# An empty step between row transposes and the next projection job in an attention loop, with weight splits and closing additions moved apart

## The reference

```python
h = rms_norm(x, g_mix_norm[l])
z = h @ w_in[l]                       # q, compressed, selected and window keys/values, gates, zu, zv
...
o_attn = gates[0] * o_cmp + gates[1] * o_sel + gates[2] * o_win      # sparse attention, 8 heads
...
o_mix = zu * sv.reshape(B, S, MIX_WIDTH)                             # gMLP groups
o = concatenate([rms_norm(o_attn, g_out[l, :ATTN_WIDTH]), rms_norm(o_mix, g_out[l, ATTN_WIDTH:])])
x = x + o @ w_out[l]
h = rms_norm(x, g_ffn_norm[l])
x = x + square(relu(h @ w_ff1[l])) @ w_ff2[l]
```

## Time and profile before

| | us |
|---|---|
| median of three runs | 595.13 |
| the profiled execution's own time | 593.15 |
| its span on the core | 591.4 |
| PE busy | 570.4 (96%) |
| DVE busy | 440.8 (75%) |
| ACT busy | 358.7 (61%) |
| POOL busy | 127.1 (21%) |

### The profile page before, as it was taken

One profiled execution on the slowest core, in us unless ns is written; L12 is line 12 of the kernel. 1 busy time (PEld: TensorE's weight loads), 2 busy tenths in 40 slices (PEclk: granted clock), 3 DMA queues, 4 the chain that ended last, 5 costly groups with the idle time before them and its releaser, 6 DMA issues.

```text
span 591.4 us, 9215 instructions
## 1 busy us (share of the span) xinstructions
PE 570.4 (96%) x3433; PEld 497.8 (84%) x3433; DVE 440.8 (75%) x721; ACT 358.7 (61%) x644; POOL 127.1 (21%) x209
## 2 busy tenths in 40 slices
PE   8999999998899979989999999999999999999997
PEld 7777777887777867878999999999998888888886
DVE  3799881685778877756967675557699996898674
ACT  6866562638676775655683377743597656556551
POOL 1550000003343533420320201321023123020200
PEclk9999999999999999999999999999999999999999
DMA  8933247251112111001998966996879889976862
GB/s 307 335 99 130 86 147 279 72 212 40 63 45 71 37 37 37 2 1 36 182 198 206 169 208 150 189 199 167 203 137 190 207 171 207 245 137 224 187 203 108
DMA packets 25164, 87.56 MB, mean 148 GB/s; under 512 B 3024, under 2 KB 3312, under 8 KB 25120
## 3 DMA queue, kind: packets, MB, share of 16 engines
q0 software_dynamic: 9856, 35.38, 32.4%
q1 hardware_dynamic: 15120, 51.59, 25.1%
q10 hardware_dynamic: 144, 0.00, 0.0%
HBM read 84.87 MB, written 2.10 MB: 147 GB/s over the span
## 4 chain that ended last, share of the span: by engine, by line
PE 81%; DVE 8%; POOL 3%; DMA 3%; ACT 2%; issue 2%; SPq 1%; DVEq 0%; ACTq 0%
PE ps L427 23%; PE ps L429 23%; PE ps L428 23%; PE ps L2057 2%; PE ps L2076 1%; DMA xT<-in_xt 1%; PE ps L1927 1%; DMA pe_sb<-in_cmp_pe 1%; PE ps L1784 1%; DVE w_lo_sb L1203 1%; DVE ps L1505 1%; PE ps L2019 1%; PE ps L2018 1%; POOL rope_k L606 1%; DVE pt_sb L1528 1%
## 5 line engine op out<-in xcount | busy, mean ns | idle before, releaser
L1039 ACT ACTIVATE w_hi_sb<-raw 128x1024 fp32r<-128x1024 f32 x112 | 118.7, 1061 | 114.8 <-PE ps L429 93.3
L1566 DVE TENSOR_TENSOR w_lo_sb<-raw,w_hi_sb 128x1024 fp32r<-128x1024 f32 x112 | 137.1, 1225 | 64.7 <-ACT w_hi_sb L1039 64.5
L680 POOL DMA_DIRECT2D raw<-in_w_ff x64 | 55.4, 865 | 237.6 <-DVE w_lo_sb L1566 213.2
L427 PE MATMUL ps<-w_hi_sb,ht_hi 128*128 128x512 f32 x192 | 78.9, 411 | 9.4 <-DVE ht_lo L1232 7.1
L427 PE MATMUL ps<-w_hi_sb,a_hi 128*128 128x512 f32 x224 | 87.1, 389 | 0.0
L428 PE MATMUL ps<-w_lo_sb,a_hi 128*128 128x512 f32 x224 | 87.1, 389 | 0.0
L429 PE MATMUL ps<-w_hi_sb,a_lo 128*128 128x512 f32 x224 | 87.1, 389 | 0.0
L427 PE MATMUL ps<-ht_hi,w_hi_sb 128*128 128x256 f32 (+1 forms) x272 | 79.1, 291 | 0.0
L429 PE MATMUL ps<-ht_hi,w_lo_sb 128*128 128x256 f32 (+1 forms) x272 | 78.8, 290 | 0.0
L428 PE MATMUL ps<-ht_lo,w_hi_sb 128*128 128x256 f32 (+1 forms) x272 | 78.7, 290 | 0.0
L429 PE MATMUL ps<-w_hi_sb,ht_lo 128*128 128x512 f32 x192 | 75.7, 394 | 0.0
(11 more groups left out here) (239 smaller groups left out, 1138.7 us busy)
## 6 DMA issues: line engine op xcount, KB each, us to landing
raw<-in_w_ff POOLq DMA_DIRECT2D x64, 512.0 KB, 6.4
raw<-in_w_ff SPq DMA_DIRECT2D x48, 512.0 KB, 3.9
raw<-in_w SPq DMA_DIRECT2D x23, 512.0 KB, 4.5
xs<-in_x SPq DMA_DIRECT2D x8, 512.0 KB, 7.7
raw<-in_cmp_w SPq DMA_DIRECT2D x8, 512.0 KB, 4.3
xT<-in_xt SPq DMA_DIRECT2D x3, 512.0 KB, 8.8
raw<-in_w_c SPq DMA_DIRECT2D x4, 304.0 KB, 2.8
out_y<-xs SPq DMA_DIRECT2D x2, 512.0 KB, 3.1
```

Source lines behind the costliest of these rows:

```text
L427: pe.matmul(out, l_hi, r_hi, start=start, stop=False)
L680: pool.dma_start(raw[:, n % RAW, :], (w_ff1, w_ff2)[stage - 1][k, q], accum_op=ALU.add, max_dma_last_dim=8192).then_inc(raw_added[n % RAW] ...
L1039: act.activation(w_hi_sb[:, FS[j], :], raw[:, j, :], ACT.Copy).then_inc(w_hi, 1)
L1566: dve.tensor_tensor(w_lo_sb[:, FS[j], :], raw[:, j, :], w_hi_sb[:, FS[j], :].bitcast(F32), ALU.subtract).then_inc(w_lo, 1)
```

## The change

The steps of the jobs are set anew: after each of the six row transposes in the loop (steps 1, 35, 41, 47, 53, 59) one step has no job, and the last projection runs in steps 61 to 64 instead of 56 to 59. The weight splits `hi` and `lo` move to steps with equal distances. `combine` is cut into its two additions, the second one step later; three readers of its result move one step with it. The sum of squares and the row scaling of tile 1's MLP input move to step 60.

```diff
 JOBS = {("mix", 3, 0): 1}
-JOBS.update({("mixo", t, 0): 2 + 4 * t for t in range(NT)})
-JOBS.update({("mixo", t, 1): 18 + 4 * t for t in range(NT)})
+JOBS.update({("mixo", t, 0): 3 + 4 * t for t in range(NT)})
+JOBS.update({("mixo", t, 1): 19 + 4 * t for t in range(NT)})
...
-                if v in (24, 40, 56):
+                if v in (25, 41, 57):
                     inverse_root("attn", v // 16 - 1, 1)
...
-                if s == 2:
-                    hi(22)
-                if s == 10:
-                    hi(23)
-                if s in (19, 22, 26, 28):
-                    hi(24 + (19, 22, 26, 28).index(s))
-                if s in (20, 36, 52):
+                if s in (3, 7, 19, 23, 27, 31):
+                    hi(22 + (3, 7, 19, 23, 27, 31).index(s))
+                if s in (21, 37, 53):
                     act.wait_ge(o_evac, 2 * (s // 16))
                     norm_sum("attn", s // 16 - 1, scr[:, 0:AW])
...
-                if s in (48, 58):
-                    t = (s - 48) // 10
+                if s in (48, 60):
+                    t = (s - 48) // 12
...
-            def combine(t, q):
+            def combine(i, e):
-                i = 2 * t + q
+                t, q = i // 2, i % 2
...
+                if e == 0:
+                    dve.wait_ge(co_done[t // 2], t % 2 + 1)
+                    dve.wait_ge(back_done, 2 * i + 2)
+                else:
+                    dve.wait_ge(o_step, i + 1)
+                dve.tensor_tensor(o, o, ps[:, 7, :].rearrange("p (h e d) -> p h e d", e=2, d=HD)[:, :, e, :], ALU.add
+                                  ).then_inc(o_evac if e else o_step, 1)
...
-                if s == 3:
-                    lo(22)
-                if s == 11:
-                    lo(23)
-                if s in (20, 23, 27, 29):
-                    lo(24 + (20, 23, 27, 29).index(s))
+                if s in (4, 8, 20, 24, 28, 32):
+                    lo(22 + (4, 8, 20, 24, 28, 32).index(s))
...
-                if s >= LAG + BACK and (s - LAG - BACK) % 8 == 7:
-                    combine((s - LAG - BACK) // 16, (s - LAG - BACK) // 8 % 2)
-                if s in (41, 48, 53, 57):
-                    ffn_rows(s // 50, {41: 0, 48: 1, 53: 0, 57: 1}[s])
+                for e in range(2):
+                    i, at_group = divmod(s - LAG - BACK - e, 8)
+                    if i >= 0 and at_group == 7:
+                        combine(i, e)
+                if s in (41, 48, 53, 60):
+                    ffn_rows(s // 50, {41: 0, 48: 1, 53: 0, 60: 1}[s])
```

More of the change, by code:

```diff
@@ L204 @@
 JOBS = {("mix", 3, 0): 1}
-JOBS.update({("mixo", t, 0): 2 + 4 * t for t in range(NT)})
-JOBS.update({("mixo", t, 1): 18 + 4 * t for t in range(NT)})
-JOBS.update({("attn", 0, 0): 34, ("attno", 0, 0): 36, ("attn", 1, 0): 40, ("attno", 0, 1): 41, ("ffn", 0, 0): 45,
-             ("attno", 1, 0): 46, ("ffn", 0, 1): 50, ("attno", 1, 1): 51, ("attn", 2, 0): 55,
-             ("attno", 2, 0): 56})
+JOBS.update({("mixo", t, 0): 3 + 4 * t for t in range(NT)})
+JOBS.update({("mixo", t, 1): 19 + 4 * t for t in range(NT)})
+JOBS.update({("attn", 0, 0): 35, ("attno", 0, 0): 37, ("attn", 1, 0): 41, ("attno", 0, 1): 43, ("ffn", 0, 0): 47,
+             ("attno", 1, 0): 49, ("ffn", 0, 1): 53, ("attno", 1, 1): 55, ("attn", 2, 0): 59,
+             ("attno", 2, 0): 61})
 def steps_of(k):
@@ L1536, in coefs @@
                 dve.reciprocal(coef[:, t, hs, b:b2 + 1], psum_p[:, t, hs, b:b2 + 1]).then_inc(coef_made, 1)
-            def combine(t, q):
-                i = 2 * t + q
+            def combine(i, e):
+                t, q = i // 2, i % 2
                 o = o_sb[:, t, 256 * q:256 * q + 256].rearrange("p (h d) -> p h d", d=HD)
-                src = ps[:, 7, :].rearrange("p (h e d) -> p h e d", e=2, d=HD)
-                dve.wait_ge(co_done[t // 2], t % 2 + 1)
-                dve.wait_ge(back_done, 2 * i + 2)
-                dve.tensor_tensor(o, o, src[:, :, 0, :], ALU.add).then_inc(o_step, 1)
-                dve.wait_ge(o_step, i + 1)
-                dve.tensor_tensor(o, o, src[:, :, 1, :], ALU.add).then_inc(o_evac, 1)
+                if e == 0:
[5 more added lines that the diff above has]
+                                  ).then_inc(o_evac if e else o_step, 1)
             def add(kind, t, h):
@@ L1567, in unit_lo @@
                                   ALU.subtract).then_inc(w_lo, 1)
-            for w in range(NV + LEAD + LAG + BACK):
+            for w in range(NV + LEAD + LAG + BACK + 1):
                 s = w - LEAD
```

## The result

The changed kernel takes 584.39 us (median; 584.14 to 585.47), the kernel before beside it 594.83 us (594.32 to 595.3): a ratio of 0.9828, 95% interval 0.9811 to 0.9845. Forecast were 590.1 us and 586.2 to 594.5. The profiled execution of the changed kernel took 584.51 us, its span is 582.8 us.

The account below looks back on a forecast made before the run. TensorE, busy 570.4 of the 591.4 us span, was taken as the bound. Terms of -5.5 us, with 0.5 given back, made 588.15 us; 1.98 us added for the median gave 590.1 us, range 586.2 to 594.5.

Parts of the forecast that it names:

- 1.98 us: Median of the runs above the profiled execution in the kernel before, added to 588.15 us to give 590.1 us.
- step 35: Transpose in attn tile 0: a new wait behind the split now at step 32, 1.1 us, between 0 and 1.5.
- all waits covered: Rival: readings find engines free, only tile 0's new waits and under 2 us elsewhere stay; -8.5 us, 586.6 us; chance 0.17.
- the empty steps: Behind the loop's transposes: a step without a job gives TensorE 2.56 us of cover in tile 2, 2.77 in tile 3.
- the end of the loop: Steps 60 to 63: three waits, 1.1 us, go with chunks in 61 to 64; 0.1 us added for the last addition.
- Steps 47 and 1: Waits for transpose readings: 2.29 us falls to 1.4 at step 47, 1.97 to 1.85 at step 1.
- Tile 0 and tile 1: Tile 0: GpSimd waits of 1.9 us go, three waits for additions, 2.1 us, come; tile 1: 2.2 us for 2.33.
- The allowance of 0.5 us: Given back on the summed gain of 5.5 us, since less idle time leaves VectorE less in which to catch up.
- The fall at 222 us: Clock drop to 0.50 behind step 47's wait of 2.29 us: gone once the wait is cut, 1.65 us back.
- GpSimd late by the splits: Rival: TensorE waits for each scaling pair blocked by a split, 4.6 us of gain lost; 594.2 us; chance 0.17.
- Late reciprocals behind the additions: Rival at VectorE's even steps: thirteen additions expose 0.6 us each, 7.8 us against 5.5 saved; 597.4 us; chance 0.08.
- The clock's return: Rival: the clock drop comes back behind another wait, 1.65 us; 591.8 us; chance 0.08.

Follow-up runs that it names:

- combine whole: The changed kernel with combine in one piece again and its three readers one step earlier; 584.68 us, ratio 0.9853 to the kernel before.
- the one with the split a step later: The changed kernel with every job behind step 1's transpose and the six weight splits one step later; 586.42 us, ratio 0.9885 to the kernel before.
- splits alone: The kernel before with only the new steps of the weight splits; 597.71 us, ratio 1.0070 to the kernel before.
- old splits: The changed kernel with the six weight splits at their old steps; 587.98 us, ratio 0.9907 to the kernel before.
- late jobs alone: The kernel before with the new table only for jobs from step 34 on; 585.73 us, ratio 0.9870 to the kernel before.
- the kernel with 2.75 us: The changed kernel with step 47's transpose moved to 48, so its projection follows at once; 588.86 us, ratio 0.9915 to the kernel before.
- jobs alone: The kernel before with the whole new job table, splits and combine unchanged; 587.05 us, ratio 0.9882 to the kernel before.
- first half alone: The changed kernel with the jobs from step 35 on as before; 594.59 us, ratio 1.0013 to the kernel before.
- mirror: The changed kernel with the eight mixo projections and the six weight splits one step earlier; 584.58 us, ratio 0.9841 to the kernel before.
- combine alone: The kernel before with only combine cut into two additions a step apart, its three readers one step later; 594.01 us, ratio 1.0004.
- old parity: The changed kernel with the eight mixo projections one step earlier, ending at odd steps, splits unmoved; 590.85 us, ratio 0.9936 to the kernel before.

## Why the gain was twice the forecast

Two steps failed. Most of the waits came as forecast, but the prediction carried 1.98 us over to the changed kernel that were falls of the clock (2.1 us of the 5.7 missing), and it charged TensorE with a wait at step 35 that isn't there (1.1 us of the 2.7 missing in idle time). The first alone decides: without the 1.98 us the range would have been 584.2 to 592.5 us, which holds the 584.39, and the rival "all waits covered" had -8.5 us for the profiled execution, where -8.6 was measured.

**What bounds it, the empty steps, the end of the loop: right.** From step 48 to the tail the named waits are gone (forecast 0.3 us left), the idle time fell from 4.74 to 1.18 us, 1.04 of it the `combine` wait of the tail in both kernels. Steps 47 and 1: forecast 1.4 and 1.85 us, measured 0.92 and 1.67. The reading behind step 47's transpose ended 3.9 us from its last matmul, not 4.2, and TensorE came for it 3.0 us from there, not 2.8.

**The step that failed in the waits: step 35.** "I take 1.1 us in all here" for the split of step 32. There is no wait. VectorE and TensorE:

```profile
193.68 1.52 DVE L1199 SCALAR_TENSOR_TENSOR w_lo_sb<-raw,gcol_sb,w_hi_sb 128x512 fp32r<-128x512 f32 x2
...
197.65 0.60 PE L1779 MATMUL ps<-ident,o_sb 128*128 128x128 f32 x4
...
199.57 0.69 DVE L1228 TENSOR_TENSOR ht_lo<-ps,ht_hi 128x512 fp32r<-128x512 f32 x1
...
200.40 0.47 PE L427 MATMUL ps<-w_hi_sb,ht_hi 128*128 128x512 f32 x1
```

The reading ends at 200.26, 0.14 us before TensorE comes. VectorE is busy without a gap from the split on, as I had said, but its queue is in the order of the steps, and TensorE itself isn't free earlier. I charged VectorE's backlog to TensorE without setting it against the cover that I had just counted (2.56 us; here TensorE came 2.3 us behind the transpose); the whole reading took 2.2 us. How near it is shows in the run with combine whole (0.21 us) and in the one with the split a step later (0.37 us).

**Tile 0 and tile 1: size.** The three new waits were there, 0.59, 0.60 and 0.38 us (1.57) for 2.1; GpSimd's 1.9 us went as forecast. First stretch 3.24 us for 3.9, second 2.08 for 2.2. In tile 1 TensorE waited for VectorE's `_lo` (0.63, 0.50, 0.31 us) and then for ScalarE's `ot_keep` (0.18, 0.18, 0.29), never for a closing addition. That the shift of the projections would cost 2.1 us was seen; that the splits' new steps are its condition was not. Without them and the cut of `combine` the same table is 2.7 us slower in its median, some 1.8 at full clock; without the table they cost 3.8 us. I priced split by split and had not asked how far each stands from the next addition.

**Idle time in sum:** -6.5 us where the terms had -3.8 (steps 0 to 15 -0.6 for 0; 16 to 31 -0.25 for -0.1; 32 to 47 -2.1 for -0.4; from 48 on -3.6 for -3.3).

**The allowance of 0.5 us** "in which VectorE catches up" had no row, and went the wrong way. TensorE's busy time in the loop fell from 108.46 to 105.99 us; the clock is 1.7 of it. Some of the other 0.8 is in the first matmul behind a wait, which shows 0.50 us for 0.39; the rest stays open. Before the loop and in the tail 0.4 us were added. Profiled execution against profiled execution that is -8.6 us: 593.15 to 584.51.

**The step that failed in the clock: one fall was counted, and there were two.** The fall at 222 us went, 1.65 us as forecast. But I added 1.98 us, the median over the profiled execution, to the changed kernel as if it were an overhead. It is no property of the launch: the changed kernel's median is 0.1 us below its profiled execution. This is 2.1 us of the 5.7 missing, the rest are the 2.7 of idle time, the 0.5 of allowance and the 0.8 less 0.4 us. The first three executions of the kernel before have no clock on record, but in the later sets 43 of 71 have the clock of two falls, and the two profiled ones had one. So the 1.98 us were most likely a second fall, behind the waits in tile 0, that the profiled execution happened not to have. By the executions at full clock, of different sets, the two kernels lie some 7 us apart (591.4 to 591.6 against 584.1 to 584.5, one 585.5); the other 3 of the 10.4 us between the medians fit two falls of the clock that went. In the last set, where the changed kernel had one fall in each execution that counts, the gain was 8.3 us by the medians.

**Readings.** VectorE's idle share in the four stretches of the earlier trace rows is 36, 20, 23 and 29%, not 18 to 30; the first stretch sums to 3.96 us, not 3.9; in the third the terms add up to a gain of 0.4 us, which is written as -0.4. None of it changes the forecast by more than 0.1 us.

**The rivals.** The nearest was "all waits covered", 586.6 us; the covered step 35 is its mechanism. GpSimd late by the splits: the scaling beside a split does take longer, and nobody waits for it. The timeline of the changed kernel:

```profile
185.52 1.60 POOL L670 TENSOR_SCALAR p_sb<-p_sb,coef,glog 128x256 f32<-128x256 f32 x2
...
186.09 1.57 DVE L1199 SCALAR_TENSOR_TENSOR w_lo_sb<-raw,gcol_sb,w_hi_sb 128x512 fp32r<-128x512 f32 x2
```

1.60 us against 1.09. I had all six pairs 0.93 us longer, and found three longer by 0.5 (1.60, and 1.41 twice in tile 0 for 0.88); the splits themselves took 1.52 to 1.67 us beside a scaling and 1.41 without. That it would cost TensorE 4.6 us is refuted. With the rule in the Trainium skill, "SBUF — State Buffer", section "SBUF: two separate sides", the longer scaling agrees. Late reciprocals behind the additions: no wait for GpSimd in the changed kernel, refuted. The clock's return: not at 222 us in any profiled execution, where the wait was cut. At 148 us it fell in kernels with the changed kernel's first steps, though not in its own two profiled executions near 584.5 us. By the recorded clock it did return in four of the seven executions of the changed kernel in the later sets; that it was at 148 us there too is likely and not shown.

## What to carry to other kernels

Where a helper engine's instruction is as long as a step (here 1.5 us in steps of 1.4 to 1.6), set it two steps ahead of the one that the bottleneck waits for, not one, and move both together: the splits alone cost 3.8 us and the projections of the first half without the splits some 2 (0.9907, old splits, against 0.9870, late jobs alone), where the pair gained 2.5 at most. Where the median of a kernel with long waits lies above its profiled execution, don't carry the difference over; look at the mean clock of its timed executions, and compare kernels at the same clock. A wait of about 2 us on TensorE can cost some 1.7 us more behind it, not each time. Before charging a backlog, subtract the cover.

## What the hardware showed unexpectedly

- In the one profiled execution with a wait of 2.75 us the clock was low for some 7 us, in those with 2.29 to 2.62 us for some 3.4. Most timed executions of the kernel with 2.75 us lost no more than those with 2.29.
- With the same waits of 1.13 and 0.54 us near 146 us the clock fell in the profiled executions of three kernels (jobs alone, first half alone, old splits), of which the second has the changed kernel's own code up to there, and not in those of five others. With 1.97 us there it fell in three (splits alone, mirror, late jobs alone) and not in four (before twice, combine alone, old parity). It also fell once near 178 us, behind a wait of 1.80.
- One execution of the changed kernel took 3001.2 us. Its record shows the granted clock at 1.00 and TensorE busy for 2993.7 us instead of 567.6. The mean matmul of its large groups is 3.4 to 4.3 times as long, while VectorE's instructions kept their length. From the page, the busy times and two groups with busy, mean ns:

```profile
PE 2993.7 (100%) x3433; PEld 2314.0 (77%) x3433; DVE 452.0 (15%) x721; ACT 364.8 (12%) x644; POOL 121.8 (4%) x209
...
L427 PE MATMUL ps<-w_hi_sb,ht_hi 128*128 128x512 f32 x192 | 337.8, 1759 | 0.0
L1563 DVE TENSOR_TENSOR w_lo_sb<-raw,w_hi_sb 128x1024 fp32r<-128x1024 f32 x112 | 137.2, 1225 | 1283.5 <-ACT w_hi_sb L1039 1283.5
```

In the first profiled execution of the changed kernel that L427 group has a mean of 410 ns, and L1563 one of 1224. No run here shows what did it.
